# The beginning of a two-block transformer kernel: part of the first loads moved from SyncE's DMA queue to ScalarE's, and the rotation angles computed after the first two weight units

## The reference

```python
def rope_tables(positions, dim):
    half = dim // 2
    inv_freq = ROPE_THETA ** (-jnp.arange(half, dtype=jnp.float32) / half)
    ang = positions.astype(jnp.float32)[..., None] * inv_freq
    return jnp.cos(ang)[:, :, None, :], jnp.sin(ang)[:, :, None, :]
```

## Time and profile before

| what | value |
|---|---|
| median of three runs | 1925.85 us |
| the profiled execution's own time | 1923.9 us |
| its span (first to last instruction) | 1921.4 us |
| TensorE matmul busy | 1867.4 us, 97% of the span |
| VectorE, ScalarE, GpSimd busy | 61%, 46%, 5% |
| TensorE busy in the first 60 us | 47.98 us |
| data moved in the first 60 us | 14.55 MB, mean 243 GB/s |

### The profile page before, as it was taken

The page is one execution under the profiler, slowest core; times in us unless marked ns, Lnnn a source line. Parts: engine busy times, 40 slices in busy tenths (PEclk is TensorE's granted clock), DMA queues, the critical chain, the costliest instruction groups (busy, mean ns, idle before and its releaser), DMA issues.

```text
span 1921.4 us, 22445 instructions
## 1 busy us (share of the span) xinstructions
PE 1867.4 (97%) x9135; PEld 1537.9 (80%) x9135; DVE 1168.7 (61%) x1352; ACT 883.3 (46%) x1063; POOL 104.1 (5%) x129
## 2 busy tenths in 40 slices
PE   7989999999899999999999999999999999999997
PEld 5877888878778887888878878887888878878886
DVE  4787554757775547456566675556456566675445
ACT  5555444555454445344355434443344355434442
POOL 5220100021100000000000000000000000000000
PEclk9999999999999999999999999999999999999999
DMA  7415876553155556663555746564663555655562
GB/s 248 160 45 157 234 217 209 198 167 125 37 189 194 178 174 209 214 214 102 157 188 181 237 163 215 179 218 165 212 217 101 154 191 182 232 168 166 181 218 92
DMA packets 194613, 340.47 MB, mean 177 GB/s; under 512 B 9550, under 2 KB 59630, under 8 KB 194512
## 3 DMA queue, kind: packets, MB, share of 16 engines
q1 hardware_dynamic: 188944, 327.76, 52.1%
q0 software_dynamic: 5568, 11.30, 2.8%
HBM read 333.24 MB, written 5.77 MB: 176 GB/s over the span
## 4 chain that ended last, share of the span: by engine, by line
PE 86%; DVE 7%; DVEq 3%; ACT 3%; issue 1%; DMA 1%; SPq 0%; ACTq 0%
PE G L709 19%; PE G L710 19%; PE G L716 19%; PE T L764 5%; PE A L709 4%; PE A L710 4%; PE A L716 4%; PE G L726 2%; PE G L727 2%; PE G L732 2%; PE T L813 1%; DVE wlo L1703 1%; ACT arena L1234 1%; PE A L726 1%; PE A L732 1%
## 5 line engine op out<-in xcount | busy, mean ns | idle before, releaser
L1703 DVE TENSOR_TENSOR wlo<-raw,whi 128x2048 fp32r<-128x2048 f32 (+3 forms) x290 | 623.8, 2154 | 517.7 <-ACT whi L1234 517.6
L1234 ACT ACTIVATE whi<-raw 128x2048 fp32r<-128x2048 f32 (+3 forms) x290 | 521.3, 1800 | 520.0 <-PE G L716 453.2
L709 PE MATMUL G<-whi,XH 128*128 128x512 f32 (+1 forms) x1392 | 550.9, 396 | 1.2 <-DVE arena L1795 1.2
L710 PE MATMUL G<-whi,XL 128*128 128x512 f32 (+1 forms) x1392 | 540.9, 389 | 0.0
L716 PE MATMUL G<-wlo,XH 128*128 128x512 f32 (+1 forms) x1392 | 342.4, 388 | 0.0
L709 PEld LDWEIGHTS G<-whi,XH 128*128 128x128 f32 x1392 | 261.5, 188 | 55.1 <-issue 2.3
L710 PEld LDWEIGHTS G<-whi,XL 128*128 128x128 f32 x1392 | 261.6, 188 | 52.8 <-issue 1.9
L716 PEld LDWEIGHTS G<-wlo,XH 128*128 128x128 f32 x1392 | 260.8, 188 | 52.8
L764 PE MATMUL T<-ident,arena 128*128 128x128 f32 x804 | 113.3, 280 | 14.7 <-ACT arena L1234 9.9
L764 PEld LDWEIGHTS T<-ident,arena 128*128 128x128 f32 x804 | 93.8, 143 | 33.7 <-issue 12.6
L1234 ACT ACTIVATE arena<-T 128x512 f32<-128x512 f32 (+2 forms) x92 | 45.9, 549 | 157.3 <-PE T L764 157.3
(11 more groups left out here) (253 smaller groups left out, 2347.9 us busy)
## 6 DMA issues: line engine op xcount, KB each, us to landing
raw<-in_w_in SPq DMA_DIRECT2D x110, 1024.0 KB, 7.5
raw<-in_w_mlp_up SPq DMA_DIRECT2D x32, 1024.0 KB, 5.2
raw<-in_w_mlp_down SPq DMA_DIRECT2D x32, 1024.0 KB, 5.7
raw<-in_w_ffn_gate SPq DMA_DIRECT2D x44, 512.0 KB, 4.1
raw<-in_w_ffn_up SPq DMA_DIRECT2D x44, 512.0 KB, 5.1
raw<-in_w_out SPq DMA_DIRECT2D x16, 1024.0 KB, 5.0
raw<-in_w_ret_proj SPq DMA_DIRECT2D x16, 1024.0 KB, 5.1
raw<-in_w_ffn_down SPq DMA_DIRECT2D x28, 512.0 KB, 3.6
```

Of the source, the lines that this page charges most:

```text
L709: nc.tensor.matmul(dst(m), hx[:, k0 + k, rows], hi[:, k, :], start=first and k == 0, stop=False)
L710: nc.tensor.matmul(dst(m), lx[:, k0 + k, rows], hi[:, k, :], start=False, stop=False)
L1234: return nc.scalar.activation(out_, in_, func, **kw)
L1703: tt(lo_, src, hi.bitcast(F32), ALU.subtract).then_inc(part_sem(blk, c, s_lo, s_lo1), 1)
```

## The change

Ahead of the weights SyncE issues only X[:, 0]. ScalarE issues the other four loads at the top of its list. On ScalarE `hi` of unit 1 and `row_hi` of tile 1 move ahead of the wait for the angles. On VectorE `angles()` moves behind `row_los` of tile 1, and the wait for X[:, 1] moves behind `row_los` of tile 0.

```diff
 @block.sync
             xrows = a["x"].rearrange("b (m p) d -> p (b m) d", p=P)
-            first(ident[:], a["c_ident"], s_xin)
             first(X[:, 0], xrows[:, 0], s_xin)
-            for n, name in enumerate(("norm_pre_mix", "norm_pre_mlp")):
-                first(rowgain[n * DEPTH * KB:(n + 1) * DEPTH * KB], a[name].rearrange("l (k p) -> (l k) p", p=P), s_gin)
-            first(X[:, 1], xrows[:, 1], s_xin1)
 @block.scalar
+            act.dma_start(ident[:], a["c_ident"]).then_inc(s_xin, 16)
+            for n, name in enumerate(("norm_pre_mix", "norm_pre_mlp")):
+                act.dma_start(rowgain[n * DEPTH * KB:(n + 1) * DEPTH * KB],
+                              a[name].rearrange("l (k p) -> (l k) p", p=P)).then_inc(s_gin, 16)
+            act.dma_start(X[:, 1], a["x"].rearrange("b (m p) d -> p (b m) d", p=P)[:, 1]).then_inc(s_xin1, 16)
             act.sem_inc(s_exp.sem, s_exp.credit)
 
             act.wait_ge(s_pre, 1)
             row_hi(0, 0, 0, 0, pre[:, 0, 0])
             hi(0, 0, 0, 0)
+            hi(0, 0, 0, 1)
+            row_hi(0, 0, 0, 1, pre[:, 0, 0])
             act.wait_ge(s_ang, 1)
             act_(cosd[:], sind[:], ACT.Sin, scale=0.5)
             act.drain()
             act_(sind[:], sind[:], ACT.Sin).then_inc(s_sin, 1)
-            hi(0, 0, 0, 1)
-            row_hi(0, 0, 0, 1, pre[:, 0, 0])
 @block.vector
-            angles()
-            dve.wait_ge(s_xin1, 16)
-            dve.sem_inc(s_x.sem, 2)
             nc.vector.tensor_copy(identb[:], ident[:])
             dve.drain()
 ...
             row_los(0, 0, 0, 0, pre[:, 0, 0])
+            dve.wait_ge(s_xin1, 16)
+            dve.sem_inc(s_x.sem, 2)
             los(0, 0, 0, 0, 1)
             row_los(0, 0, 0, 1, pre[:, 0, 0])
+            angles()
```

## The result

The changed kernel takes 1932.35 us (median of 7 runs, 1931.41 to 1933.65), the kernel before, run beside it, 1925.85 us (median of 7, 1922.99 to 1927.68). The ratio is 1.0037, with a 95% interval of 1.0027 to 1.0047: about 7 us slower. The forecast was +4.85 us and 1930.7. The profiled execution took 1932.97 us with a span of 1930.4, against 1923.9 and 1921.4 before: 9.0 more.

What follows compares the result with a forecast made beforehand. TensorE's steady stream was taken as the bound, set by when unit 2 starts (30.42), where two paths meet. Terms -1.5 - 0.8 + 5.2 + 1.95 = +4.85 us gave a median of 1930.7, range 1926.5 to 1933.8.

Steps and rivals of the forecast that it cites:

- step 4: ScalarE's path to unit 2: Squares wait for the moved angles and Sins, starting at 29.62 instead of 24.38; 5.2 us lost.
- step 5: TensorE before unit 2: idle for 5.2 us, then a restart at the lower clock costing 1.95.
- Rival A: TensorE's clock does not fall in the stall, or only for a moment; +2.9, time 1928.7; chance 0.2.
- steps 1 to 3: The start: earlier loads, unit 0 straight behind the small product at 13.55 (1.5 us won), earlier clock rise (0.8 won).
- the "nothing" for the four issues on ScalarE: Four load issues of 0.42 each on ScalarE lie under its wait for the first transpose and cost nothing.
- rival B: Loads win nothing, unit 0 lands near 13.0; +7.2, 1933 to 1934.3; counterargument: earlier issue, engines idle for 2 us; chance 0.15.
- 2.3 was to be won: TensorE's whole path up to tile 1 moves ahead by 1.5 + 0.8 = 2.3 us.
- step 3: TensorE's clock rises sooner because the small product runs straight into unit 0; 0.8 us won, bounds 0 and 1.95.
- the 11.2 that was taken: Landing of unit 0's raw data, issued at 1.17 with 10.0 us to land; bounds 9.8 and 13.0.
- step 6: GpSimd's and VectorE's rotations, which wait for the Sin ending at 27.3, and the moved X[:, 1] wait: cost nothing.
- Its 1.95 below the median: The profiled execution's own time, 1923.9, lies 1.95 below the runs' median; used to turn 1928.8 into 1930.7.

Runs made afterwards that it cites:

- Experiments 2: The kernel before with only the changed orders on ScalarE and VectorE, its loads kept; 1932.12 us, ratio 1.0036 to the kernel before.
- 8: The changed kernel with VectorE's angles behind the reciprocal and ScalarE's Sins behind the high parts of units 2 and 3; 1927.72 us, ratio 1.0007 to before.
- Experiments 6 and 7: The changed kernel with 20, then 12, unread matmuls put in TensorE's stall before unit 2; 1933.95 and 1931.54 us, ratios 1.0045 and 1.0027 to before.
- the four other kernels with these loads: The loads moved alone (ratio 0.9998), and the changed kernel with 20 matmuls in the stall (1.0045), with 12 (1.0027), or with late angles (1.0007).
- experiment 4: The changed kernel with SyncE waiting for both gain vectors before it issues unit 0's weights; one run, 1931.03 us.
- experiment 3: The changed kernel with the identity and both gain vectors back on SyncE's queue ahead of the weights; ratio 1.0041 to the kernel before.
- experiment 9: The kernel before with only X[:, 1] issued behind unit 0 instead of ahead of it; ratio 0.9994.
- the best kernel: Late angles, gains ahead of X[:, 0], X[:, 1] behind unit 0, GpSimd's loads reordered; run twice, 1923.78 and 1923.60 us, ratios 0.9991 and 0.9989 to before.

## Why the prediction was right, and where not

**The path to unit 2 (step 4): right.** The mechanism, its place and its size. The angles took 3.01, the two Sins 0.79; the Squares moved from 24.38 to 31.53, 7.15, of which 2.17 is the later start; so 4.98 against 5.24. The small gaps that were added, 0.07 and 0.05, are not there: XL and the angles, and the Sin and the Squares, overlap by 0.09 each, with a gap of 0.03 between the angles and the Sin. The table load was covered. Experiments 2 and 8 show the cause: with this order alone the loss is there, with the angles elsewhere the stall is gone.

**The stall and the clock (step 5): right.** Idle 4.8 against 5.2, and 2.24 for the restart against 1.95. Experiments 6 and 7 show that it is the idle stretch that costs it: 5.54 and 5.58 for unit 2 with the stretch filled or cut to 2.0, against 7.80. The granted clock of 0.50 behind it says the same. Rival A, the clock staying up, is out. That the price of the start was so near is partly luck: unit 0's slow stretch made its half unit 4.6 to 5.3 us long from one kernel to the next.

**The start (steps 1 to 3): wrong.** "TensorE's start at 7.11 moves to between 5 and 7.1" was the step that failed: it went to 10.16, and to 9.17 to 9.40 in the four other kernels with these loads. It was argued from the gains' place on a shorter queue alone, and the "nothing" for the four issues on ScalarE counted only the issuing. Competition with unit 0's packets was weighed for X[:, 1] and not for the gains; experiment 4 shows that it is what delays them. Nor were the engines idle in the hole at 5.0, as rival B's counterargument has it. So 2.3 was to be won, and the profile lost 1.9 at unit 0 and 0.25 more up to tile 1; the small product ran from 12.45 to 14.34, was over before unit 0's high part was made, and decided nothing.

The 0.8 for an earlier rise of the clock (step 3) had no ground either. It hung on a short gap before unit 0, and where the gap was shorter, 0.61 in experiment 3 and 0.85 in experiment 9, the half unit at the low pace still took 5.10 and 5.15, against 4.84 before with 1.57.

The terms as the profile has them, 2.17 + 4.98 + 2.24 = 9.4, give the delay of 9.3 at unit 3, where the forecast had 4.85. The whole miss is the start's. It looks smaller in the median, 1932.35 against 1930.7, than in the span, 1930.4 against 1926.3, and that is luck: the changed kernel's profile had the latest start of five, and the profiled execution of before was a fast one (below). Rival B's sum (+7.2) meets the 7.1 of the runs, by another mechanism: the weights did land earlier, and the rows did not. The weights' landing itself came at 11.5, near the 11.2 that was taken. The rule of the Trainium skill (DMA: Bandwidth & Descriptors, "Issuing engines are not separate DMA queues"), that a second issuer saves only issue time, gives that 11.2, and the trace agrees; that the sharing can also delay a small transfer was not drawn from it. Here the second gain vector took 7.4 to 8.4 us in the five profiles, against 4.9 before.

**What hangs on the Sin (step 6): right for this order.** GpSimd's rotation began at 42.10 instead of 38.35, and TensorE never waited for it: the delay of 9.33 at unit 3 is 9.1 at the end. In experiment 8, where the Sin ends at 35.7 and not at 31.6, it cost 0.7.

**The profiled execution as the base.** Its 1.95 below the median was taken for a constant. It goes with the clock: over the 29 runs of before beside the last three kernels, those with a mean granted clock of 0.997 or more took 1921.9 to 1925.6 us, those with 0.995 or less 1925.3 to 1929.7. The profiled one had 0.997. So the distance of the two profiles, 9.0, is 2 more than the runs say, 7.1.

## What to carry to other kernels

Before an instruction is moved out of an engine's idle slot, look at what stands behind the new place in the list of the engine that waits for it: three microseconds of vector work that were free became five on the path, and TensorE's pause took two more by its clock. A small load that the first work needs belongs ahead of the large ones in time, not only on another queue; the second queue gave it no precedence here, and two small loads from a third, GpSimd's, held both up. Where two paths meet within a few tenths, as at 30.4 here, a shortcut on one of them is worth nothing and a delay on either is paid in full.

## What the runs showed that was not expected

- A load of 8 KB took from 1.8 to 8.4 us to land, by what the other queues moved at the time: 1.8 ahead of everything, 4.1 with the weights held back, 7.4 to 8.4 beside them.
- The time of single runs of the kernel before differs by up to 8 us (1921.9 to 1929.7), and goes with the mean granted clock. In the two profiles of the best kernel, 1927.35 and 1923.03 us, the clock fell for longer in the attention stretches of the slower one: 0.86 against 0.94 from 125 to 155, and 0.88 against 0.95 from 500 to 535.
- Where VectorE's and GpSimd's arithmetic ran side by side, the one that started second took longer in two places. VectorE's subtraction of 128 x 2048, started at 56.02 behind a GpSimd product of 55.99 in experiment 8, took 3.40 instead of 2.31 us. In the kernel before, GpSimd's sum, started at 49.93 behind a VectorE subtraction of 49.87, took 3.36 instead of 1.29, and the subtraction its usual 2.27.
